# Feed-forward of a two-layer decoder trunk: gate and up tiles of two of its three segments as seven block products of 256 tokens

## What is computed

```python
for i in range(DEPTH):                      # DEPTH = 2, D_MODEL = 1024, SEQ = 512
    h = rmsnorm(x, norm1[i])
    ...                                     # mixer i and memory cross-attention
    x = x + jnp.concatenate([mix, xo], axis=-1) @ w_out[i]
    h = rmsnorm(x, norm2[i])
    gu = h @ w_gate_up[i]                   # (512, 1024) @ (1024, 2 * 2816)
    x = x + (jax.nn.silu(gu[..., :2816]) * gu[..., 2816:]) @ w_down[i]
```

## Time and profile before

| | |
|---|---|
| median of 3 runs | 1234.74 us (1234.59 to 1235.09) |
| span of the profiled execution | 1232.9 us |
| TensorE busy (matmuls) | 1227.6 us, 5846 matmuls |
| TensorE weight loads | 1004.2 us |
| GpSimd busy | 843.5 us |
| VectorE busy | 520.5 us |
| ScalarE busy | 360.6 us |
| granted TensorE clock | 1.000 |

### The profile page before, as it was taken

How to read it: one execution, slowest core, us unless ns; L and a number is a source line. 1 busy time by engine, 2 the same in 40 slices (tenths; PEclk the granted TensorE clock), 3 DMA queues, 4 the chain that set the end, 5 groups by cost and what they waited for, 6 DMA issues and landing times.

```text
span 1232.9 us, 16216 instructions
## 1 busy us (share of the span) xinstructions
PE 1227.6 (100%) x5846; PEld 1004.2 (81%) x5846; DVE 520.5 (42%) x795; ACT 360.6 (29%) x716; POOL 843.5 (68%) x1029
## 2 busy tenths in 40 slices
PE   9999999999999999999999999999999999999998
PEld 8888877788888888888888777778888888888887
DVE  6954444644232233112345888884423113221331
ACT  6523456633220011001241666655222001100110
POOL 7997433567777787777776544436778777777775
PEclk9999999999999999999999999999999999999999
DMA  7334111123223232232243222222323323322223
GB/s 273 99 129 143 64 52 52 52 86 104 93 102 102 85 102 93 95 102 98 77 132 103 70 69 71 70 69 70 100 87 100 103 85 102 102 89 100 97 71 105
DMA packets 35067, 117.01 MB, mean 95 GB/s; under 512 B 4417, under 2 KB 4930, under 8 KB 34886
## 3 DMA queue, kind: packets, MB, share of 16 engines
q1 hardware_dynamic: 33416, 112.83, 27.5%
q10 hardware_dynamic: 1598, 3.51, 1.1%
HBM read 111.07 MB, written 2.11 MB: 92 GB/s over the span
## 4 chain that ended last, share of the span: by engine, by line
PE 97%; DVE 2%; ACT 1%; issue 0%; ACTq 0%; POOL 0%; DVEq 0%; POOLq 0%
PE PS L1552 95%; PE PS L1952 1%; DVE Al L1280 0%; PE PS L1795 0%; PE PS L1980 0%; DVE nmB L1456 0%; PE PS L1921 0%; PE PS L1905 0%; PE PS L1913 0%; PE PS L1620 0%; DVE PB L1468 0%; DVE Al L1380 0%; ACT tmp L801 0%; ACT tmp L809 0%; DVE PB L1467 0%
## 5 line engine op out<-in xcount | busy, mean ns | idle before, releaser
L574 POOL TENSOR_TENSOR w_lo<-w_raw,w_hi 128x256 fp32r<-128x256 f32 (+1 forms) x800 | 616.1, 801 | 17.0
L569 POOL TENSOR_SCALAR w_hi<-w_raw 128x1024 fp32r<-128x1024 f32 (+2 forms) x204 | 214.7, 1052 | 357.2 <-PE PS L1552 357.1
L1552 PE MATMUL PS<-Hh,w_hi 128*128 128x512 f32 x1072 | 428.0, 399 | 0.0
L1552 PE MATMUL PS<-Hh,w_lo 128*128 128x512 f32 x1072 | 418.0, 390 | 0.0
L1552 PE MATMUL PS<-Hl,w_hi 128*128 128x512 f32 x1072 | 417.7, 390 | 0.0
L1552 PEld LDWEIGHTS PS<-Hh,w_hi 128*128 128x128 f32 x1072 | 201.3, 188 | 47.8 <-issue 8.2
L1552 PEld LDWEIGHTS PS<-Hh,w_lo 128*128 128x128 f32 x1072 | 201.2, 188 | 42.7
L1552 PEld LDWEIGHTS PS<-Hl,w_hi 128*128 128x128 f32 x1072 | 201.5, 188 | 39.3 <-issue 1.0
L1552 PE MATMUL PS<-Ah,w_hi 128*128 128x512 f32 (+1 forms) x544 | 207.9, 382 | 0.1
L1552 PE MATMUL PS<-Ah,w_lo 128*128 128x512 f32 (+1 forms) x544 | 205.0, 377 | 0.0
L1552 PE MATMUL PS<-Al,w_hi 128*128 128x512 f32 (+1 forms) x544 | 205.0, 377 | 0.0
(11 more groups left out here) (263 smaller groups left out, 995.5 us busy)
## 6 DMA issues: line engine op xcount, KB each, us to landing
w_raw<-in_wt_dram SPq DMA_DIRECT2D x181, 512.0 KB, 3.3
w_raw<-in_wt_dram SPq DMA_DIRECT2D x16, 384.0 KB, 3.0
w_raw<-in_wt_dram SPq DMA_DIRECT2D x8, 448.0 KB, 3.2
QKR<-QKP ACTq DMA_DIRECT2D x24, 128.0 KB, 4.3
xT<-in_x_t_dram SPq DMA_DIRECT2D x8, 256.0 KB, 5.5
out_dram<-xT SPq DMA_DIRECT2D x8, 256.0 KB, 2.0
mT<-in_mem_t_dram SPq DMA_DIRECT2D x1, 1024.0 KB, 10.1
cn<-in_constants_dram SPq DMA_DIRECT2D x1, 594.5 KB, 7.6
```

The costliest lines, as they stand in the source:

```text
L569: nc.gpsimd.tensor_scalar(w_hi[:, sl, 0:nk], w_raw[:, raw, 0:nk], 0.0, 1.0, ALU.add, ALU.mult).then_inc(w_round, 1)
L574: lo = nc.gpsimd.tensor_tensor(w_lo[:, sl, w], w_raw[:, raw, w], w_hi[:, sl, w].bitcast(F32), ALU.subtract)
L1552: return nc.tensor.matmul(out_, a, b, start=start, stop=stop)
```

## The change

It sets `SEG = [(0, 6), (6, 8), (14, 8)]`. Segment 0 stays as it was, with six pairs. In segments 1 and 2 a pair of gate and up tiles is one 2x2 block matrix (gate, up by the low and high four input blocks), the normed activations are another (low and high input blocks by the first and last 256 tokens), and their product is taken in Winograd's form of Strassen's method: seven products instead of eight, each of four blocks, three passes and 256 tokens, 84 matmuls for a pair instead of 48 of 512 tokens. There are 16 such pairs in a layer, 32 in all. The products are q0 to q6, in PSUM banks `Q_BANK`; q4, q5 and q6 are accumulated on top of q0, q2 and q3.

- Activations: during segment 0 VectorE makes the normed tokens (`normed`, eight operations), their four sums (`tokens_sum`, 128x1024) and the seven `lo` (`tokens_lo`, 128x1024), ScalarE the seven `hi` (`tokens_hi`). They serve all 16 pairs of the layer.
- Weights, for each pair: GpSimd makes four sums of 128x512 (`weight_sums`) and two of the seven `lo` (q1, q2; 128x512), ScalarE the seven `hi` (128x512), VectorE the other five `lo` (q0, q3, q4, q5, q6). They are made for pair i+1 while TensorE works on pair i. GpSimd has no rounding to do there any more.
- Out of PSUM, for each pair: ScalarE copies q0 (`P1_COPY`), VectorE makes five sums of 256 columns, ScalarE two SiLUs of 256 columns, VectorE the product, ScalarE Ah, VectorE Al.
- Entry: the last two down tiles ahead of a segment of pairs ("shared tiles") are rounded by ScalarE; GpSimd makes the `lo` of their first four blocks, VectorE of the rest. GpSimd makes three of the next pair's sums ahead of the `lo` of the second shared tile.
- The loops of the feed-forward are written out where pairs are, so there are more instructions. Some buffers move in SBUF, some semaphores are merged (the four rows of `m_rows` have one, so `head_diag(0)` waits for all four), the angles are made in other buffers, and `wz_raw` is loaded after another wait.

The core of the diff:

```diff
-SEG = [(0, 8), (8, 8), (16, 6)]
+SEG = [(0, 6), (6, 8), (14, 8)]
...
+Q_BANK = [2, 3, 4, 6, 2, 4, 6]
+GATE_BANK, HID_BANK = 5, 7
+V_LO = [0, 3, 4, 5, 6]
+V_ENTRY = [4, 6, 0, 5, 3]
+P_LO = [1, 2]
+HI_ENTRY = [4, 6, 0, 1, 5, 2, 3]
...
+def low_count(p, q):
+    return len(V_LO) * p + SHARED * entries(p) + (V_ENTRY if is_entry(p) else V_LO).index(q) + 1
+def lows_of(p):
+    return len(V_LO) * (p + 1) + SHARED * entries(p)
...
+        def pair_source(n, q):
+            gate, up = w_raw[:, n % RAW], w_raw[:, (n + 1) % RAW]
+            return (gate[:, 0:4], W_SUM[1], W_SUM[0], W_SUM[2], gate[:, 4:8], W_SUM[3], up[:, 4:8])[q]
...
                 nk = tile_k(n)
-                if n >= RAW:
-                    sp.wait_ge(w_split, n - (RAW - 1))
+                if n >= RAW and pair_at(n - RAW):
+                    sp.wait_ge(s_low_v, lows_of(pair_number(*pair_at(n - RAW))))
+                elif n >= RAW:
+                    sp.wait_ge(w_split, PLAIN[n - RAW] + 1)
+                    if shared_tile(n - RAW):
...
+            def weight_sums(n, p, first, last):
+                gate, up = w_raw[:, n % RAW], w_raw[:, (n + 1) % RAW]
+                if first == 0:
+                    loaded(n)
+                    loaded(n + 1)
+                    if p % NSP == 0:
+                        pool.wait_ge(f_ready, HC * (p // NSP) + NS)
+                    if p:
+                        pool.wait_ge(s_low_p, 2 * p)
+                    nc.gpsimd.tensor_tensor(W_SUM[0], up[:, 0:4], up[:, 4:8], ALU.add).then_inc(s_add, 1)
+                    pool.wait_ge(s_add, 4 * p + 1)
+                    nc.gpsimd.tensor_tensor(W_SUM[1], W_SUM[0], gate[:, 0:4], ALU.subtract).then_inc(s_add, 1)
+                    if p:
+                        pool.wait_ge(s_low_v, max(low_count(p - 1, 3), low_count(p - 1, 5)))
+                    nc.gpsimd.tensor_tensor(W_SUM[2], gate[:, 0:4], up[:, 0:4], ALU.subtract).then_inc(s_add, 1)
+                if last == 4:
+                    pool.wait_ge(s_add, 4 * p + 2)
+                    nc.gpsimd.tensor_tensor(W_SUM[3], gate[:, 4:8], W_SUM[1], ALU.subtract).then_inc(s_add, 1)
+            def weight_low(n, p, q):
+                b = block_of(pair_at(n)[0], q)
+                pool.wait_ge(s_round, weight_round(p, q))
+                nc.gpsimd.tensor_tensor(wq_lo[:, b:b + 4], pair_source(n, q), wq_hi[:, b:b + 4].bitcast(F32),
+                                        ALU.subtract).then_inc(s_low_p, 1)
             for n in range(2, N_TILES):
+                at = pair_at(n)
+                if at:
+                    if (n - seg_base(at[0], at[1])) % 2 == 0:
+                        weight_sums(n, pair_number(*at), 3 if at[2] == 0 else 0, 4)
...
+                    pool.wait_ge(product, 6 * pair_number(l, s, SEG[s][1] - 1) + (4 if n % 2 else 2))
+                elif T_OUT[1] <= n < T_OUT[1] + 3:
                     pool.wait_ge(dense_done, T_HEAD if n == T_OUT[1] else n - 2)
                 elif T_OUT[1] + 3 <= n < T_OUT[1] + KD:
                     pool.wait_ge(out_open, n - T_OUT[1] - 1)
                 elif n >= SPLIT:
                     pool.wait_ge(dense_done, used_for(n))
+                if shared_tile(n):
+                    if shared_tile(n)[1] == SHARED - 1:
+                        weight_sums(n + 1, shared_tile(n)[0], 0, 3)
+                    pool.wait_ge(s_round, shared_round(n))
+                    for i, done in ((0, w_first), (2, w_split)):
+                        nc.gpsimd.tensor_tensor(w_lo[:, sl, i:i + 2], w_raw[:, raw, i:i + 2], w_hi[:, sl, i:i + 2].bitcast(F32),
+                                                ALU.subtract).then_inc(done, 1)
...
+                def weight_hi(s, i, q):
+                    n, p, b = seg_base(l, s) + 2 * i, pair_number(l, s, i), block_of(l, q)
+                    if q in (0, 4, 6):
+                        m = n + (q == 6)
+                        act.wait_ge(w_in[m % RAW], (m // RAW + (m % RAW > 0)) * 16)
+                    else:
+                        act.wait_ge(s_add, 4 * p + {1: 2, 2: 1, 3: 3, 5: 4}[q])
+                    if i and q == 6:
+                        act.wait_ge(dense_done, n)
...
+                def shared_hi(n):
+                    act.wait_ge(w_in[n % RAW], (n // RAW + (n % RAW > 0)) * 16)
+                    act.wait_ge(dense_done, used_for(n))
+                    nc.scalar.activation(w_hi[:, slot_of(n), 0:tile_k(n)], w_raw[:, n % RAW, 0:tile_k(n)],
+                                         ACT.Copy).then_inc(s_round, 1)
...
+                def pair(s, i):
+                    h, p = SEG[s][0] + i, pair_number(l, s, i)
+                    more = i + 1 < SEG[s][1]
+                    act.wait_ge(product, 6 * p + 1)
+                    if p:
+                        act.wait_ge(joined, joined_of(p - 1, 1))
+                    nc.scalar.activation(P1_COPY, PS[:, Q_BANK[0], 0:HALF_T], ACT.Copy).then_inc(gate_read, 1)
+                    if more:
+                        for q in range(4):
+                            weight_hi(s, i + 1, q)
+                    act.wait_ge(product, 6 * p + 5)
+                    nc.scalar.activation(PS[:, GATE_BANK, 0:HALF_T], PS[:, Q_BANK[4], 0:HALF_T], ACT.Silu).then_inc(gate_read, 1)
+                    if more:
+                        weight_hi(s, i + 1, 4)
+                        weight_hi(s, i + 1, 5)
+                    act.wait_ge(joined, joined_of(p, 4))
+                    nc.scalar.activation(PS[:, GATE_BANK, HALF_T:SEQ], C12, ACT.Silu).then_inc(silu_done, 1)
+                    if more:
+                        weight_hi(s, i + 1, 6)
+                    act.wait_ge(gu_ready, n0 + h + 1)
+                    nc.scalar.activation(Ah[:, i], PS[:, HID_BANK], ACT.Copy).then_inc(f_hi, 1)
+                gate_silu(0)
...
+                def normed(k0, k1):
+                    dve.wait_ge(joined, tokens_of(l, 1))
+                    for k in range(k0, k1):
+                        a, b = (tmp4, k // 2) if k < 4 else (PS, k // 2)
+                        dst = a[:, b:b + 3:2, k % 2 * HALF_T:(k % 2 + 1) * HALF_T]
+                        nc.vector.scalar_tensor_tensor(dst, xT[:, k].rearrange("p (h n) -> p h n", h=2), col(R_N2 + 8 * l + k),
+                                                       PS[:, SS_BANK].rearrange("p (h n) -> p h n", h=2),
+                                                       ALU.mult, ALU.mult).then_inc(joined, 1)
+                def tokens_sum(j):
+                    q, a, b, op, need = ((3, T_SRC[5], in_tmp(2), ALU.subtract, 9), (2, in_tmp(2), in_tmp(0), ALU.subtract, 9),
+                                         (1, T_SRC[3], in_tmp(0), ALU.add, 11), (6, T_SRC[4], T_SRC[1], ALU.subtract, 12))[j]
+                    dve.wait_ge(joined, tokens_of(l, need))
+                    nc.vector.tensor_tensor(T_SRC[q], a, b, op).then_inc(joined, 1)
+                def tokens_lo(j):
+                    q = T_ORDER[j]
+                    dve.wait_ge(s_round, token_round(l, j))
+                    nc.vector.tensor_tensor(as_quarter(tc_lo[:, q]), T_SRC[q], as_quarter(tc_hi[:, q].bitcast(F32)), ALU.subtract)
+                def shared_lo(n):
+                    sl, raw, nk = slot_of(n), n % RAW, tile_k(n)
+                    dve.wait_ge(s_round, shared_round(n))
+                    nc.vector.tensor_tensor(w_lo[:, sl, 4:nk], w_raw[:, raw, 4:nk], w_hi[:, sl, 4:nk].bitcast(F32),
+                                            ALU.subtract).then_inc(s_low_v, 1)
...
+                def pair(s, i):
+                    n, h, p = seg_base(l, s) + 2 * i, SEG[s][0] + i, pair_number(l, s, i)
+                    more = i + 1 < SEG[s][1]
+                    def low(*qs):
+                        if more:
+                            for q in qs:
+                                weight_low(s, i + 1, q)
+                    def part(q):
+                        return PS[:, Q_BANK[q], 0:HALF_T]
+                    low(0)
+                    dve.wait_ge(gate_read, 2 * p + 1)
+                    dve.wait_ge(product, 6 * p + 2)
+                    nc.vector.tensor_tensor(U_SUM, part(1), P1_COPY, ALU.add).then_inc(joined, 1)
+                    dve.wait_ge(product, 6 * p + 3)
+                    dve.wait_ge(joined, joined_of(p, 1))
+                    nc.vector.tensor_tensor(W_JOIN, part(2), U_SUM, ALU.add).then_inc(joined, 1)
+                    dve.wait_ge(product, 6 * p + 4)
+                    dve.wait_ge(joined, joined_of(p, 2))
+                    nc.vector.tensor_tensor(UP[:, HALF_T:SEQ], part(3), W_JOIN, ALU.add).then_inc(joined, 1)
+                    low(3, 4)
+                    dve.wait_ge(product, 6 * p + 6)
+                    nc.vector.tensor_tensor(C12, part(5), U_SUM, ALU.add).then_inc(joined, 1)
+                    low(5)
+                    dve.wait_ge(dense_done, n + 2)
+                    nc.vector.tensor_tensor(UP[:, 0:HALF_T], part(6), U_SUM, ALU.add).then_inc(dense_free, 2)
```

(75 more changed lines are left out.)

324 lines of the change are left out of this document (241 added, 83 removed).

## The result

The changed kernel takes 1214.89 us (median of 4 runs, 1213.84 to 1215.02), the kernel before 1234.84 beside it. The ratio is 0.9836, with a 95% interval of 0.9822 to 0.9850. The prediction was 1216.1 with a range of 1209 to 1231. The profiled execution took 1213.84 us for a span of 1212.0; before, the span was 1232.9. So the span fell by 20.9 us where 18.6 were forecast.

The account below looks back on a forecast made before the run. TensorE was taken to bound the kernel. 25.6 us gained in the pairs less 7.0 at the entries gives 18.6, from 1232.9 to 1214.3; the median lies 1.8 above, so 1216.1, range 1209 to 1231.

Parts of the forecast that it names:

- TensorE's step: Block products in the pairs: 0.120 us per 256-column matmul (bounds 0.113 and 0.192), 10.08 us a pair, 25.6 us gained.
- Entries: TensorE waits for GpSimd at the second shared down tile, 2.4 and 1.1 us, two layers: 7.0 us lost.
- GpSimd: Per pair, six 128x512 operations, slowdown beside five `lo`s and own waits: 9.8 us, hidden barely under TensorE's 10.08.
- VectorE: Per pair, five `lo`s at 1.17 us, five sums, product, Al and gaps: 9.8 us of 10.08, delays absorbed.
- ScalarE: Roundings, copy, SiLUs and Ah in each pair: 6.9 us of 10.08.
- DMA: Later raw weight loads in each pair land at about 8.3 us: cost 0; 0.3 to 1 if transfers are in line.
- segment 0: VectorE's 19 more operations a layer, 21 us beside six pairs: cost 0; without that cover 1 us a layer.
- moved things: Down tiles, the row loads' one semaphore, `wz_raw`, the angles and written-out loops: cost 0.
- GpSimd binds: Rival in the pairs: GpSimd's operations take 1.35 us, a pair 10.35; 1224.7 us, chance 0.22.
- The lock at full price: Rival in the pairs: each VectorE `lo` costs GpSimd its whole 0.62 us, 10.9 a pair; 1241 us, chance 0.06.
- VectorE binds: Rival at each pair's five `lo`s: at 1.5 us each a pair takes 11.43; 1259 us, chance 0.10.
- Entries hidden: Rival at the entries to segments of pairs: their waits are hidden; 1209.1 us, chance 0.07.

Follow-up runs that it names:

- no turns: Changed kernel, but VectorE's five `lo` subtractions for the next pair read PSUM instead of the raw tile or sum, one SBUF operand each: 1211.84 us (one execution).

## Why the prediction was right

**TensorE's step, the mis-sized term.** Forecast 0.120 from the earlier trace rows, measured 0.1178 in every pair: 9.893 instead of 10.08, a gain of 31.6 instead of 25.6. The form was right and the bound of 0.113 held it, but the step goes with the operands' buffer, and the rows were of another one. It is 6.0 us, the largest error. Weight loads of 188 ns overlap as those of the earlier trace rows did.

**Entries.** Forecast 2.4 and 1.1 us in two layers, 7.0; measured 2.67 and 1.52, 3.12 and 1.53, 8.84. Place, cause (three sums ahead of the `lo`s) and size were right. The two 256-column subtractions took 1.85 against 1.45, as VectorE was beside them. Not foreseen was that the longer gap costs clock, 1.5 us. Together 3.3 us more were lost than forecast. In the span the error of 2.3 us (1214.3 forecast, 1212.0 measured) is 6.0 and the 0.4 of the stage between in one direction, 3.3 and the unassigned 0.7 in the other: errors that partly cancelled. In the median it is 1.2, since the three other runs took 1.0 to 1.2 us longer than the profiled one. Their mean granted clock is 0.997 against 0.999. In the traces of three experiments with the same entries and a mean of 0.997 (no turns, and the two that read `Hh` and `Hl`), TensorE drops to 1.2 GHz after segment 0 of layer 0 too, where the profiled execution didn't. So one more drop is the likely cause; the rows of the three runs themselves aren't there to show it. That the forecast of the median was off by only 1.2 is partly luck.

**GpSimd.** Forecast 9.8, measured 9.80. An operation in a stream takes 1.27, as forecast: without turns the period is 7.88, of which 0.25 are waits for its own results, and the rest over six is 1.27. A `lo` beside it costs 0.38, against 0.40, and 0.25 stand against the 0.2 set aside. "Hidden, barely" was right, and tighter than forecast, since TensorE's step is quicker: 0.09 of room where the forecast had 0.3.

**VectorE.** Forecast 1.17 a `lo`, measured 1.22 and 1.28; its sum is 9.06 of 9.893. It didn't bind, even with one operation more.

**ScalarE, DMA, segment 0, moved things.** ScalarE has 5.6 of at most 6.9. No pair inside a segment waits for a transfer, TensorE has no new gap in segment 0, and the segments' new lengths cost nothing by themselves. All at 0, as forecast.

**The rivals.** GpSimd binds: fell by 0.09 us a pair, and one operation of 0.74 more made it true. The lock at full price: fell. GpSimd gives up 0.38 for each `lo` in the pairs, where the operation alone steps by 0.62. The rule of the Trainium skill (SBUF — State Buffer, section "SBUF: two separate sides") has VectorE's `lo` wait for GpSimd and the other way round, each for the whole instruction; this trace agrees on who waits (a `lo` takes 1.22 to 1.28 against 0.69 with one SBUF operand) and not on the whole price. VectorE binds: fell. Entries hidden: they weren't, but another order of GpSimd's sums hides nearly all of them, at 1203.84.

## What to carry to other kernels

When block products trade TensorE's work for additions elsewhere, the additions have to fit beside the quicker pair, not the old one, and must not stand in an engine's queue ahead of work that is due. Here all that was lost in waits was lost at the entries, where GpSimd, which works in order, made the next pair's sums ahead of a tile that TensorE waited for. Take a matmul's step from rows that read the same buffer, or keep a range of some per cent. And price a gap in front of TensorE with the clock behind it: one of 3.3 us took 1.5 us more. Behind a gap as long it did not happen in every execution, so such a price has a range too.
